# Norm factor behind a gate made from three sums that the linear in front collects, and all of its roots taken over columns

## The reference, cut to what matters

```python
x = x + gt_m * rmsnorm(y, g_post_mix[l])
h = modulate(x, g_pre_ffn[l], sh_f, sc_f)          # rmsnorm(x, g) * (1 + scale) + shift
x = x + gt_f * rmsnorm(swiglu(h, w_ffn_in[l], w_ffn_out[l]), g_post_ffn[l])
```

## Time and profile before

| what | us |
|---|---|
| median of 3 runs | 3340.32 (3338.01 to 3346.14) |
| the profiled execution's own time | 3341.07 |
| its span in the trace | 3339.2 |
| PE busy | 3063.7 (92%) |
| DVE busy | 1708.5 (51%) |
| POOL busy | 1050.0 (31%) |
| ACT busy | 1044.4 (31%) |

### The profile page before, as it was taken

The page is one execution under the profiler, slowest core; times in us unless marked ns, Lnnn a source line. Parts: engine busy times, 40 slices in busy tenths (PEclk is TensorE's granted clock), DMA queues, the critical chain, the costliest instruction groups (busy, mean ns, idle before and its releaser), DMA issues.

```text
span 3339.2 us, 48249 instructions
## 1 busy us (share of the span) xinstructions
PE 3063.7 (92%) x16932; PEld 2473.9 (74%) x16936; DVE 1708.5 (51%) x2815; ACT 1044.4 (31%) x1847; POOL 1050.0 (31%) x573
## 2 busy tenths in 40 slices
PE   6778779999998899899998997899999999899997
PEld 3655658888886766799895765788877866688886
DVE  4755768865335566443245766342343347643423
ACT  3145131121114265422224324422223226532222
POOL 1121213223322411344443420344445301244443
PEclk9879989999999899999999998999999969999999
DMA  6200413433211101222222210232224100022222
GB/s 241 78 1 7 151 57 126 164 132 132 82 52 43 51 1 34 69 92 94 89 87 66 76 38 1 92 100 95 94 84 120 55 13 2 20 95 95 94 94 82
DMA packets 74344, 258.83 MB, mean 78 GB/s; under 512 B 9456, under 2 KB 12016, under 8 KB 72688
## 3 DMA queue, kind: packets, MB, share of 16 engines
q1 hardware_dynamic: 60256, 205.61, 18.8%
q10 hardware_dynamic: 13968, 51.65, 4.6%
HBM read 253.03 MB, written 2.10 MB: 76 GB/s over the span
## 4 chain that ended last, share of the span: by engine, by line
PE 83%; DVE 6%; issue 6%; ACT 2%; SPq 1%; ACTq 1%; DVEq 1%; PEld 1%; POOL 0%; POOLq 0%; DMA 0%; PEldq 0%
PE ps L842 56%; PE ps L808 6%; PE ps L2516 2%; PE ps L2530 2%; PE ps L426 1%; PE ps L1879 1%; PE ps L2684 1%; DVE ps L389 1%; PE ps L1114 1%; PE ps L1685 1%; PE ps L2748 1%; PE ps L1690 1%; ACT w_hi L630 1%; PEld ps L842 1%; PE ps L2669 1%
## 5 line engine op out<-in xcount | busy, mean ns | idle before, releaser
L766 POOL TENSOR_TENSOR w_lo<-w_raw,w_hi 128x1024 fp32r<-128x1024 f32 (+1 forms) x373 | 918.1, 2463 | 1800.2 <-ACT w_hi L630 1685.6
L630 ACT ACTIVATE w_hi<-w_raw 128x1024 fp32r<-128x1024 f32 (+1 forms) x373 | 386.2, 1038 | 1236.0 <-PE ps L842 996.8
L842 PE MATMUL ps<-h_hi,w_hi 128*128 128x258 f32 (+2 forms) x1824 | 329.8, 324 | 54.1 <-ACT w_hi L630 40.9
L842 PEld LDWEIGHTS ps<-h_hi,w_hi 128*128 128x128 f32 x1824 | 271.1, 192 | 89.4 <-issue 34.7
L842 PE MATMUL ps<-h_lo,w_hi 128*128 128x258 f32 (+2 forms) x1824 | 318.6, 317 | 0.0
L842 PE MATMUL ps<-h_hi,w_lo 128*128 128x258 f32 (+2 forms) x1824 | 316.4, 315 | 0.0
L842 PEld LDWEIGHTS ps<-h_lo,w_hi 128*128 128x128 f32 x1824 | 269.7, 191 | 23.8
L842 PEld LDWEIGHTS ps<-h_hi,w_lo 128*128 128x128 f32 x1824 | 267.5, 190 | 23.9
L930 DVE CAST act_hi<-f_t 128x512 f32 (+1 forms) x88 | 167.5, 1904 | 12.6
L842 PE MATMUL ps<-hb_hi,w_hi 128*128 128x512 f32 x672 | 166.7, 390 | 1.7 <-issue 1.7
L842 PE MATMUL ps<-act_hi,w_hi 128*128 128x512 f32 (+1 forms) x660 | 154.6, 375 | 14.0 <-ACT w_hi L630 13.4
(11 more groups left out here) (343 smaller groups left out, 5045.8 us busy)
## 6 DMA issues: line engine op xcount, KB each, us to landing
w_raw<-in_ffn_in SPq DMA_DIRECT2D x176, 512.0 KB, 3.4
mod_row<-in_w_mod_rows ACTq DMA_DIRECT2D x80, 512.0 KB, 4.4
w_raw<-in_ffn_out SPq DMA_DIRECT2D x64, 512.0 KB, 3.4
w_raw<-in_ev_in SPq DMA_DIRECT2D x26, 512.0 KB, 3.4
w_raw<-in_ffn_out SPq DMA_DIRECT2D x32, 384.0 KB, 3.0
w_raw<-in_od_in SPq DMA_DIRECT2D x21, 512.0 KB, 3.4
mod_ring<-in_w_mod SPq DMA_DIRECT2D x8, 1024.0 KB, 13.1
w_raw<-in_wo_in SPq DMA_DIRECT2D x12, 512.0 KB, 3.4
```

The costliest lines, as they stand in the source:

```text
L630: act.activation(k.w_hi[:, s, 0:self.KT * P], k.w_raw[:, s, 0:self.KT * P], ACT.Copy).then_inc(k.sems["w_hi_ready"], 1)
L766: ins = pool.tensor_tensor(k.w_lo[:, s, 0:self.KT * P], k.w_raw[:, s, 0:self.KT * P], k.w_hi[:, s, 0:self.KT * P].bitcast(F32), ALU.subtract)
L842: ins = pe.matmul(k.ps[:, self.step * s + g, 0:t1 - t0], w[:, s, c * P:(c + 1) * P], h[:, c, t0:t1], start=(n == 0), stop=(n == len(parts) ...
```

## The change

- A gate is `ahead` where the linear in front has no modulation rows: gates 2, 3 and 4. That linear then collects two more sums on the way. Per slab, ACT squares the slab once more with the gate's gain as its scale (`s1_sq`; two instructions for 768 tokens). DVE multiplies slab, gain and x (`s2_p`; two instructions for 768), adds that into `s2_acc` and adds `s1_sq` into `s1_acc`. Before its first slab DVE clears both accumulators and scales the gains.
- Inside these gates ACT makes no squares and PE sums none per chunk. PE instead sums `s1_acc`, the last `s1_sq`, `s2_acc` and the last `s2_p` over columns, in the gate's stage, and spreads y's factor between the first and the rest. DVE combines the sums with the mean of x² that the gate before left in `s_col`, in five small instructions after chunk 1, takes the reciprocal after chunk 3, and PE spreads the factor after chunk 4's high products; ACT copies it into `n_r` after chunk 5.
- Gate 1 keeps its squares, summed over columns. The order of the last chunk changes: the sum comes in front of its products.
- All roots of the gates and of `Norm` are taken over columns: Sqrt, reciprocal, spread.
- `w_hi` and `w_lo` of slab 1 of the next linear move into the linear in front of the gate: ACT makes it between the last two slabs' squares, and POOL makes both in `first_low`, within the linear's stage.

```diff
+def column_means(pe, k, squares, T, start=True, stop=True, bank=5, at=0):
+    for q in range(T // P):
+        ins = pe.matmul(k.ps[:, bank, at + q:at + q + 1], squares[:, q * P:(q + 1) * P], k.ones[:, 0:1], start=start and q == 0, stop=stop, skip_group_check=True)
+    return ins
+class RootColumns:
+    def y_root(self, act):
+        act.activation(k.hn_col[:, 0:n], k.ps[:, 5, 0:n], ACT.Sqrt, bias=k.eps[:, 0:1]).then_inc(k.sems["y_std"], 1)
+    def y_factor(self, dve):
+        dve.reciprocal(k.hn_rcol[:, 0:n], k.hn_col[:, 0:n]).then_inc(k.sems["y_rcol"], 1)
+    def y_spread(self, pe):
+        spread_columns(pe, k, flat(k.ps[:, 6:8]), k.hn_rcol[:, 0:n], 1, self.T).then_inc(k.sems["y_rstd"], 1)
...
+    def tensor(self, pe):
+        if not self.ahead:
+            self.y_spread(pe)
+            return
+        column_means(pe, k, k.s1_acc, T, bank=4, at=self.SELF)
+        self.y_spread(pe)
+        pe.wait_ge(k.sems["s1_ready"], a.b_s1 + a.M)
+        column_means(pe, k, k.s1_sq[:, (a.M - 1) % 2], T, start=False, bank=4, at=self.SELF)
+        column_means(pe, k, k.s2_acc, T, start=False, bank=4, at=self.CROSS)
+        pe.wait_ge(k.sems["s_op"], a.b_s + 3 * (a.M - 1) + 1)
+        column_means(pe, k, k.s2_p, T, start=False, bank=4, at=self.CROSS).then_inc(k.sems["s_mean"], 1)
...
+    def x_square(self, dve, chain):
+        chain.link(dve.tensor_tensor(t, sums(self.SELF), r, ALU.mult))
+        chain.link(dve.tensor_tensor(t, t, sums(self.CROSS), ALU.add))
+        chain.link(dve.tensor_tensor(t, t, r, ALU.mult))
+        chain.link(dve.tensor_tensor(s, s, t, ALU.add))
+        dve.tensor_scalar(s, s, 0.0, None, ALU.max).then_inc(k.sems["x_mean"], 1)
...
     def scalar(self, act, chain):
-        inverse_root(act, chain, k, r, r).then_inc(k.sems["y_rstd"], 1)
-        self.next.high(act, 1, 0, 1)
+        self.y_root(act)
...
+            if self.ahead and c == 2:
+                self.x_root(act)
+            if self.ahead and c == 5:
+                self.x_factor(act)
...
-        self.pre.act_factor(act, chain)
...
-    def gpsimd(self, pool, chain):
-        self.next.low(pool, 1, 0, 1)
...
     def square(self, act, m, e):
         act.activation(k.f_sq[:, e % 2, :T].unsqueeze(1), self.tile(m), ACT.Square, scale=D ** -0.5).then_inc(k.sems["sq_ready"], 1)
+        if self.extra:
+            for j, (t0, t1) in enumerate(self.to.groups):
+                ins = act.activation(k.s1_sq[:, e % 2, t0:t1].unsqueeze(1), self.tile(m)[:, :, t0:t1], ACT.Square, scale=k.gate_d[:, j, at])
+            ins.then_inc(k.sems["s1_ready"], 1)
...
         eng.sem_inc(k.sems[f"psum_free{s}"], 1)
+        if self.extra:
+            for j, (t0, t1) in enumerate(self.to.groups):
+                ins = eng.scalar_tensor_tensor(k.s2_p[:, t0:t1].unsqueeze(1), self.tile(m)[:, :, t0:t1], k.gate_2d[:, j, at], k.x[:, at, t0:t1], ALU.mult, ALU.mult)
+            ins.then_inc(k.sems["s_op"], 1)
         if last and self.to:
             return
+        if self.extra:
+            eng.tensor_tensor(k.s2_acc[:, :T], k.s2_acc[:, :T], k.s2_p[:, :T], ALU.add).then_inc(k.sems["s_op"], 1)
         eng.wait_ge(k.sems["sq_ready"], m + (self.b_sq + 1))
         eng.tensor_tensor(k.n_acc[:, :T], k.n_acc[:, :T], k.f_sq[:, e % 2, :T], ALU.add).then_inc(k.sems["sq_used"], 1)
+        if self.extra:
+            eng.wait_ge(k.sems["s1_ready"], m + (self.b_s1 + 1))
+            eng.tensor_tensor(k.s1_acc[:, :T], k.s1_acc[:, :T], k.s1_sq[:, e % 2, :T], ALU.add).then_inc(k.sems["s_op"], 1)
...
-                act.preload_act_table_set("natural_log")
+                act.preload_act_table_set("sqrt_and_others")
             for e in range(2):
+                if isinstance(self.to, Gate) and e == 1:
+                    self.to.next.high(act, 1, 0, 1)
                 split(self.M - 2 + e, self.M - 2 + e)
...
-            self.to.next.low(pool, 0, 0, 0)
+            self.to.next.first_low(pool)
...
-            means(pe, k, 6, k.f_sq[:, (self.M - 1) % 2], self.T, start=False).then_inc(k.sems["y_mean"], 1)
+            column_means(pe, k, k.f_sq[:, (self.M - 1) % 2], self.T, start=False).then_inc(k.sems["y_mean"], 1)
```

More of the change, by code:

```diff
@@ L179, with __init__ @@
 class Pre:
-    def __init__(self, kit, cols, shift, groups, hi, lo, twice=False):
+    def __init__(self, kit, cols, shift, groups, hi, lo, twice=False, mean=True):
         self.kit, self.cols, self.shift, self.groups, self.hi, self.lo, self.twice = kit, cols, shift, groups, hi, lo, twice
@@ L440, in __init__ @@
+class Gate(Stage, RootColumns):
+    SELF, CROSS = 0, 8
     def __init__(self, kit, groups, cols, norm_cols, shift, hi, lo, twice=False):
         super().__init__(kit)
-        self.groups, self.cols, self.T = groups, cols, groups[-1][1]
+        self.groups, self.cols, self.T, self.n = groups, cols, groups[-1][1], groups[-1][1] // P
+        self.ahead = kit.stages[-2].rows is None
         kit.stages[-2].feed(self)
-        self.b = {n: kit.reserve(n, c) for n, c in (("y_mean", 1), ("y_rstd", 1), ("gate_t", DC), ("gate_x", DC), ("sq_ready", DC), ("sq_used", DC - 1))}
@@ L486, in vector @@
             dve.tensor_tensor(k.x[:, c, :T], k.x[:, c, :T], k.n_t[:, c % 2, :T], ALU.add).then_inc(k.sems["gate_x"], 1)
+            if self.ahead and c == 1:
+                self.x_square(dve, chain)
+            if self.ahead and c == 3:
+                self.x_reciprocal(dve)
         self.pre.dve_lo(dve, DC - 1)
-    def gpsimd(self, pool, chain):
-        self.next.low(pool, 1, 0, 1)
-class Norm(Stage):
+        if not self.ahead:
+            self.x_square(dve, chain)
+            self.x_reciprocal(dve)
+class Norm(Stage, RootColumns):
     def __init__(self, kit, src, cols, dst):
@@ L867, in products @@
             order = []
+            squares = lambda c: (lambda: a.pe_squares(pe, c))
+            gate = isinstance(a, Gate)
             for c in range(K):
+                first = gate and not a.ahead and c == K - 1
+                if first:
+                    order.append(squares(c))
                 order += [hi_in(c), (0, 0, c), (0, 2, c), (1, 0, c), (1, 2, c)]
-                if isinstance(a, Gate):
-                    order.append(lambda c=c: a.pe_squares(pe, c))
+                if gate and not a.ahead and not first:
+                    order.append(squares(c))
+                if gate and c == (4 if a.ahead else K - 1):
+                    order.append(lambda: a.x_spread(pe))
                 order += [lo_in(c), (0, 1, c), (1, 1, c)]
@@ L942, in vector @@
         if self.feeds:
+            if self.extra:
+                dve.memset(k.s1_acc[:, :T], 0.0)
+                dve.memset(k.s2_acc[:, :T], 0.0)
+                n = len(self.to.groups)
+                dve.tensor_scalar(k.gate_d[:, 0:n], self.to.cols[:, 0:n], D ** -0.5, None, ALU.mult)
+                chain.link(dve.tensor_scalar(k.gate_2d[:, 0:n], self.to.cols[:, 0:n], 2.0 / D, None, ALU.mult))
             chain.link(dve.memset(k.n_acc[:, :T], 0.0))
@@ L2333, in memory @@
     k.act_lo = at("act_lo", [P, KMAX, TOK], F32R, A + 24576)
+    k.s1_sq = at("s1_sq", [P, 2, TOK], F32, A + 18432)
+    k.s2_p = at("s2_p", [P, TOK], F32, A + 43008)
+    k.s1_acc = at("s1_acc", [P, TOK], F32, A + 46080)
+    k.s2_acc = at("s2_acc", [P, TOK], F32, TMP + 9216)
     k.y = at("y", [P, DC, TOK], F32, Y)
```

83 lines of the change are left out of this document (65 added, 18 removed).

## The result

The changed kernel took 3365.02 us, median of 4 runs (3363.10 to 3370.30), against 3340.38 for the kernel before: ratio 1.0076, 95% interval 1.0063 to 1.0088, so slower by 0.8%, and 7.7 us above the forecast of 3357.3. Its profiled execution took 3363.10, with a span of 3361.2, 22.0 more than before.

What follows compares the result with a forecast made beforehand. PE was taken to bound the kernel (83% of the chain). Linears +36.3 us and gates -19.3 on 3341.07 gave 3358.1, or 3357.3 against the median, slower; likeliest case 3349 to 3375, range 3332 to 3376 for all but hidden sums.

Steps and rivals of the forecast that it cites:

- I take POOL's part and these four as excluding each other: Linears: POOL's weight part and DVE's new operations plus the n_acc add never overlap; the linears cost 36.3 us.
- hidden sums: Rival (0.16): in the linears POOL and DVE do not hold each other off; the gates' gain stands, time 3326.
- balance: Rival (0.13): about half of each collision in the linears is avoided, 18 to 20 us for them, time 3341.
- DVE's start 0.7 us later: Front of a gate: DVE starts 0.7 us later than before, relative to the end of the last eviction.
- partly beside root and reciprocal: Front of gates 2 to 4: PE's s1_acc sums, 12 or 8 records, run partly during root and reciprocal.
- The part moves ahead of the gate, so that 2.0 us goes: Front of a gate: the first x add no longer lies under POOL's w_lo, saving 2.0 us, 1.2 in gates 3 and 4.
- I charge nothing more: Meeting before a gate: POOL's second part ends about with the sums of y², no charge; up to 1.5 us if later.
- The backs: Last x add to slab 2: 5.9 us in gate 2, 4.5 in gate 3, with some 1.7 regained from the clock there.
- The factor is not what the back waits for: Rival (0.09): the next linear waits for w_hi and meeting as long as before; 15 us less gain, time 3373.
- Cold gates: Rival (0.12): PE, with gaps of 0.8 to 1.1 us in every chunk, falls to 1.2 GHz; 13 us more, time 3371.
- Sum: Whole kernel: 3341.07 + 36.3 for the linears - 19.3 for the gates = 3358.1 profiled, 3357.3 as median.

Runs made afterwards that it cites:

- psum_acc: The changed kernel with the two running sums of the linears in PSUM, only the last addition of each writing SBUF; 3338.41 us, 0.9990.
- part_back: psum_acc with s1_acc and s2_acc summed over columns before the last y squared, and POOL's part of slab 1 behind the meeting again; 3333.23 us, 0.9969.
- parts_only: The kernel before with one edit: both weight parts of slab 1 in front of the gate, all roots as they were; 3342.34 us, 0.9999.
- no_ahead: The changed kernel with all gates in gate 1's form, without the sums in the linears, squares of x back behind the chunks; 3347.5 us, 1.0018.

## Why the prediction was right in sign and short in size

- **"I take POOL's part and these four as excluding each other"**: right, and shown by psum_acc; *hidden sums* and *balance* are out. The spacings were 0.3 too long (7.55, 6.65, 6.1 for 7.21, 6.32, 5.83): POOL's part starts at 1757.50, inside the `n_acc` add and not behind it, and the held add ends 0.54 after POOL and not a full 0.69. The linears cost 28.8 instead of 36.3. *Balance* would have had 18 to 20.
- **"DVE's start 0.7 us later"**: the step that failed. It was 3.7, 2.0 and 2.0. I had the cold price of a group and let it lie "partly beside root and reciprocal"; the `s1_acc` sums stood wholly before the spread. That price came out near by luck: the 0.11 us a record of the earlier trace rows was read as the high level, but the clock was 0.50 there (the window from 176 to 179 us above), and those spreads have weights of 64 columns. The gates' spreads, with 128 columns and also at 0.50, took 2.06 for eight, 0.26 each, near the doubled figure of 0.22. Then `x_square`: five operations in 1.0 and the reciprocal in 0.2, not 2.3 for all six, but behind a wait of 1.15 and 1.3 in gates 3 and 4 that I had left out. The last x add moved by +2.3, +2.6 and +2.8 (forecast +1.0, +1.75, +1.75).
- **"The part moves ahead of the gate, so that 2.0 us goes"**: the add is short in gate 2, but part_back shows that the later start of DVE alone did that. In gates 3 and 4 the size was right (1.23) and the operation was not: it was the low part. The move itself bought nothing that shows and cost 1.9 in gate 1's linear, where I had not looked for what POOL would meet. **"I charge nothing more"** for the meeting held in the changed kernel, where Sqrt starts 0.12 behind the sums; in parts_only it cost 1.0 in gates 3 and 4.
- **The backs**: 5.7, 4.6 and 4.4 for 5.9 and 4.5, and 1.5 us a gate of clock regained for 1.7. *The factor is not what the back waits for* is out. Gates 2 to 4 gave 12.9 for 16.5, because of their fronts; gate 1 gave 0.5 for 2.5, `Norm` lost 0.3.
- *Cold gates* did not come in the changed kernel by its mechanism: in gate 2 the clock was back at 1.00 from 1055 us on, with PE idle for 2.3 of 12 us between the products. What the Trainium skill's page "TensorE: Matmul & The Clock Gate", section "A second HAM failure mode: psum-queue depth-cycling", says of short idles that come often did not show in these chunks. In no_ahead the products were cold with no gaps at all. But the gates were colder than before in their fronts: from the last eviction's end to about the end of slab 2 the mean granted clock was 0.82, 0.77 and 0.73 in gates 2 to 4, against 0.90, 0.86 and 0.85.

```profile
1060.00:1072.00 12.00, 9.73 (x58) 7.94 (x57) 10.39 (x18) 5.18 (x9) 0.00 (x0) 1.00 0.00 0
```

- **Sum**: the changed parts gave +15.7 against the forecast of +17. The two errors, linears too dear by 7.5 and gates with `Norm` too generous by 6.2 (19.3 for 13.1), nearly cancel: that the changed parts came within 1.3 us of the forecast is luck. Unchanged code added 6.3 in the profiled execution, 5.6 of it in one stage, for which the forecast had no term; the medians differ by 24.6 in one set of runs and 19.3 in the other.

## What to carry to other kernels

Before adding work to an engine that looks idle, draw one turn of its loop with the operands' places: a DVE add with both operands in SBUF beside a GpSimd operation costs up to that operation's whole length, and keeping the accumulator in PSUM takes it away with no other edit (27 us here). Shortening a chain with narrow matmuls is not free: on the same 512 tokens they needed about as long as the wide ones, and TensorE was at 1.2 GHz for much of the fronts made of them. Whatever an engine is given ahead of a meeting delays all who meet there; a moved instruction wants a look at what it meets at its new place.
